# Low halves of the weight units of both attention stages: VectorE in one instruction of 1024 columns, in place of GpSimd in two of 512

## What is computed

```python
for i in range(DEPTH):
    h = rmsnorm(x, norm_g[i])
    mem_h = rmsnorm(mem, mem_norm_g[i])
    ...
    if i % 2 == 0:
        proj = jnp.einsum('bsd,de->bse', h, w_in_a[j])
        ...
        o_mix = mixer_dilated(qkv, qn_a[j], kn_a[j], ang_a)
    else:
        proj = jnp.einsum('bsd,de->bse', h, w_in_b[j])
        ...
        o_mix = mixer_axial_gqa(proj[..., :c1], proj[..., c1:c2], proj[..., c2:c3],
                                qn_b[j], kn_b[j], ang_b)
    ...
    o_mem = memory_attention(q_mem, mem_h, w_mem_kv[i], mem_qn_g[i], mem_kn_g[i])
    y = jnp.concatenate([o_mix, o_mem], axis=-1) * jax.nn.silu(gate)
    x = x + jnp.einsum('bse,ed->bsd', y, w_out[i])
```

## Time and profile before

| | |
|---|---|
| Median of 3 runs | 3570.39 us (3569.19 to 3571.53) |
| The profiled execution | 3569.75 us |
| Its span | 3567.8 us |
| TensorE busy | 3408.9 us (96%) |
| VectorE busy | 1560.0 us (44%) |
| ScalarE busy | 1321.2 us (37%) |
| GpSimd busy | 1412.1 us (40%) |
| Mean granted TensorE clock | 0.983 of full speed |

### The profile page before, as it was taken

The page is one execution under the profiler, slowest core; times in us unless marked ns, Lnnn a source line. Parts: engine busy times, 40 slices in busy tenths (PEclk is TensorE's granted clock), DMA queues, the critical chain, the costliest instruction groups (busy, mean ns, idle before and its releaser), DMA issues.

```text
span 3567.8 us, 45553 instructions
## 1 busy us (share of the span) xinstructions
PE 3408.9 (96%) x16418; PEld 2820.1 (79%) x16418; DVE 1560.0 (44%) x2613; ACT 1321.2 (37%) x2104; POOL 1412.1 (40%) x1040
## 2 busy tenths in 40 slices
PE   8999998899999999999889999989998999999898
PEld 7888876788888888887678888878787877877677
DVE  2221456542216422145654221653785387335633
ACT  3222435442225422243544222462442244444343
POOL 5554432145544454443314554343332432352122
PEclk9999999999999999999999999999999999999999
DMA  4223221023222222221102222222111211231111
GB/s 155 97 94 99 84 65 48 19 90 99 94 96 94 83 95 99 95 85 64 53 13 94 94 95 97 99 87 78 66 60 48 82 60 54 77 130 54 42 54 59
DMA packets 76659, 281.09 MB, mean 79 GB/s; under 512 B 8512, under 2 KB 8640, under 8 KB 76128
## 3 DMA queue, kind: packets, MB, share of 16 engines
q1 hardware_dynamic: 75600, 274.66, 23.2%
q10 hardware_dynamic: 912, 4.39, 0.4%
HBM read 276.92 MB, written 2.10 MB: 78 GB/s over the span
## 4 chain that ended last, share of the span: by engine, by line
PE 87%; DVE 8%; ACT 3%; issue 2%; DMA 0%; DVEq 0%; ACTq 0%; SPq 0%
PE ps L1765 16%; PE ps L1767 16%; PE ps L1766 16%; PE ps L1837 4%; PE ps L1838 3%; PE ps L1839 3%; PE ps L2301 3%; PE ps L2287 2%; PE ps L1876 2%; PE ps L1874 2%; PE ps L1875 2%; PE ps L2227 1%; PE ps L2348 1%; PE ps L2229 1%; PE ps L2228 1%
## 5 line engine op out<-in xcount | busy, mean ns | idle before, releaser
L536 POOL TENSOR_TENSOR w_lo<-raw,w_hi 128x512 fp32r<-128x512 f32 x1028 | 1400.5, 1385 | 2132.2 <-ACT w_hi L587 2132.1
L1765 PE MATMUL ps<-x_hi,w_hi 128*128 128x512 f32 x2560 | 1049.7, 410 | 4.6 <-issue 4.6
L1767 PE MATMUL ps<-x_hi,w_lo 128*128 128x512 f32 x2560 | 1000.1, 391 | 0.0
L1766 PE MATMUL ps<-x_lo,w_hi 128*128 128x512 f32 x2560 | 999.2, 390 | 0.0
L587 ACT ACTIVATE w_hi<-raw 128x1024 fp32r<-128x1024 f32 x514 | 542.2, 1057 | 1084.3 <-PE ps L1767 596.5
L1765 PEld LDWEIGHTS ps<-x_hi,w_hi 128*128 128x128 f32 x2560 | 483.2, 189 | 126.4 <-issue 29.5
L1766 PEld LDWEIGHTS ps<-x_lo,w_hi 128*128 128x128 f32 x2560 | 483.0, 189 | 118.5 <-issue 22.4
L1767 PEld LDWEIGHTS ps<-x_hi,w_lo 128*128 128x128 f32 x2560 | 481.5, 188 | 102.1
L1204 DVE TENSOR_TENSOR T<-T,ps 128x512 f32<-128x512 f32 x88 | 60.5, 687 | 660.1 <-PE ps L1767 650.8
L708 ACT ACTIVATE T<-ps 128x512 f32<-128x512 f32 x88 | 52.6, 598 | 359.5 <-PE ps L1767 354.6
L1874 PE MATMUL ps<-h_hi,w_hi 128*128 128x512 f32 (+1 forms) x440 | 153.2, 348 | 0.0
(11 more groups left out here) (327 smaller groups left out, 5205.9 us busy)
## 6 DMA issues: line engine op xcount, KB each, us to landing
raw<-in_weights SPq DMA_DIRECT2D x514, 512.0 KB, 3.3
Y<-in_x_t SPq DMA_DIRECT2D x1, 2048.0 KB, 7.9
mem<-in_mem_t ACTq DMA_DIRECT2D x2, 1024.0 KB, 7.1
out_t<-Y SPq DMA_DIRECT2D x8, 256.0 KB, 2.2
ple_p<-in_p_t ACTq DMA_DIRECT2D x2, 512.0 KB, 5.2
mat<-in_mats SPq DMA_DIRECT2D x1, 768.0 KB, 11.7
masks<-in_masks ACTq DMA_DIRECT2D x1, 576.0 KB, 8.0
rope<-in_rope_b ACTq DMA_DIRECT2D x1, 512.0 KB, 8.6
```

The costliest lines, as they stand in the source:

```text
L536: ins = pool.tensor_tensor(g.wl[:, k, part], g.raw[:, k, part], g.wh[:, k, part], ALU.subtract)
L1765: mm(out, wh[:, c], xh[:, kc, :], start=kc == 0, stop=False)
L1766: mm(out, wh[:, c], xl[:, kc, :], start=False, stop=False)
L1767: ins = mm(out, wl[:, c], xh[:, kc, :], start=False, stop=kc == DC - 1)
```

## The change

VectorE gets its own `low(u)`: it waits for the high half of the unit, subtracts all 1024 columns in one instruction and counts `lo_ready` up. `attend` calls it as `low(op.u + 4)` for each unit of the plan, behind the groups in the unit's middle and ahead of the copy of the unit's tile. GpSimd leaves these units out: in stage A the units from the tenth to the ninth from the end (90 units), in stage B the same (30 units). Before its first, VectorE waits until GpSimd has made the units ahead; GpSimd goes on when `lo_ready` has reached the end of the stretch. The ring, the plans, ScalarE, TensorE and SP are as before.

```diff
--- before.py
+++ after.py
@@ -321,6 +321,13 @@
 
 GATES_BEFORE, EARLY = 8, 5
 
+
+def vector_units(i):
+
+    u0 = BASE["AB"][i]
+    return u0 + 10, u0 + (U_A, U_B)[i] - 8
+
+
 PLANS = (between(plan_a()), between(plan_b()))
 
 
@@ -561,6 +568,11 @@
             q = g.CV[:, 0:4, n * P:(n + 1) * P]
             pool.tensor_tensor(q, q, g.EG[:, n, :].rearrange("p (h q) -> p h q", h=4), ALU.mult)\
                 .then_inc(s.qdec_done, 1)
+    for i in range(2):
+        first, last = vector_units(i)
+        low_many(at, first)
+        pool.wait_ge(s.lo_ready, last)
+        at = last
     low_many(at, N_UNITS)
 
 
@@ -1673,8 +1685,15 @@
             v.tensor_tensor(g.OL[:, t - 1, :], g.O[:, t - 1, :], g.OH[:, t - 1, :], ALU.subtract)\
                 .then_inc(s.olo_done, 1)
 
+    def low(u):
+        k = u % RING
+        dve.wait_ge(s.hi_ready, u + 1)
+        v.tensor_tensor(g.wl[:, k, :], g.raw[:, k, :], g.wh[:, k, :], ALU.subtract).then_inc(s.lo_ready, 1)
+
     def attend(i):
         dve.wait_ge(s.arena_landed, 16 * ARENA_LANDED[i])
+        dve.wait_ge(s.lo_ready, vector_units(i)[0])
+
         def item(op):
             if isinstance(op, Group):
                 group(op)
@@ -1688,6 +1707,7 @@
                 for mid in op.mid:
                     if isinstance(mid, Group):
                         item(mid)
+                low(op.u + 4)
                 if op.kind == "a_v" and op.t % 4 == 3:
                     dve.wait_ge(s.unit_done, op.u + 1)
                     if op.t == 15:
```

## The result

The changed kernel takes **3670.07 us** (median of 4 runs, 3668.62 to 3676.03) against 3570.6 for the kernel before on the same chip: a ratio of **1.0283, 95% interval 1.027 to 1.0295**, so 99.5 us slower. The forecast was 3647, 76 us slower: the sign and the range held, the sum came out 23 us short. The profiled execution of after is the 3676.03 (span 3674.0), 6 us over its median; what is counted in its trace adds up to 106.2, not 99.5.

What follows compares the result with a forecast made beforehand. TensorE was taken as the bound, with VectorE's queue the one that must not get later; seven terms of new TensorE idle time summed to 76.2 us on the profiled 3569.75, forecast 3647 us, range 3610 to 3700.

Steps and rivals of the forecast that it cites:

- step 3: Attention A's heads, 12 places with one unit between two groups: chain 1.1 us later, wait 0.76 each, 9.1 us.
- Step 4: A's first head, a group behind each of six units: a lap takes 8.9 us against 7.63, five laps, 6.4 us.
- Step 6: b_q units of B: 0.3 us later in one unit of a pair, about 0.8 in the other; four pairs, 4.4 us.
- step 1: Units with no group behind: sum of squares waits 1.2 us in 22 places, plus mem_k and A's last mem_q; 33.4 us.
- 2 V copies: Late copies of V hold banks the next unit writes: six places in A 13.4 us, one in b_v 1.6; 15.0.
- step 5: B's units with a group in the middle: 1.0 us three times, 0.4 for b_k, 2.3 before them; 5.7 us.
- 7 gates: Gates: group about 0.1 us late, B's twelve 1.2, plus 1.0 for the norm behind each stage's gate 0; 2.2 us.
- a rival at 0.12: Clock dips of 1.7 us at one in two of some 60 new TensorE waits: 76 + 50, 3697 us; chance 0.12.
- A under 0.97: Sign that the slower clock case holds: the granted clock of attention A falls under 0.97.
- faster rival: VectorE's relief from GpSimd wins: half of TensorE's waits for L1609 go and nothing comes, 3559 us; chance 0.06.

Runs made afterwards that it cites:

- unit_earlier: Changed kernel with VectorE's low half at the same place but for unit u + 3, whose high half was made a unit ago; 3543.98 us, ratio 0.9926.
- behind_norm: Changed kernel with the low half moved in VectorE's queue behind the tile's copy and the norm of the tile before; 3559.4 us, ratio 0.9968.

## Why the prediction was right in sign and short in size

**Right.** The bound was read rightly: VectorE's queue, not its load. The copy is 2.23 us late where the forecast said 2.3; the low half takes 1.225 us for the 1.21 forecast; the counts 788 and 120 are there; the rope products are at their least (L1586, the old L1574, at 0.679 us); L2368 waits in 30 places, 12 of them for 1.01 us and nine for 1.56 to 1.70; A's idle time is 84 us for "about 90", B's 43 for "about 45". The 76.2 us of the sum were meant as idle time of TensorE, and 72.6 us of new waits came. That they lie this close is in part luck: the list holds less of each wait than it costs (see below), and without the clock's 24 the profiled difference is 82 us, 6 over the sum, with step 3 and the places of no step too short and steps 4 and 6 too long. What the sum did not hold at all is the clock.

**By the steps.** Both traces are set side by side by the start of each unit's high half (L587, L599): how far after has fallen behind before, and by how much more at each unit. By this the steps cost:

| step | forecast | measured | what made the difference |
|---|---|---|---|
| 1 sums without group | 33.4 | 40.9 | 22 places at 1.25 to 1.28 (27.8 for 26.4); mem_k 4.2 and 4.4 for 2.5 a stage; last mem_q 4.5 for 2.0 |
| 2 V copies | 15.0 | 24.6 | 2.3, 3.7, 3.9, 3.8, 3.8, 3.3, and b_v 3.8 |
| 3 pairs of groups | 9.1 | 15.8 | 1.3 each for 0.76: three units of a later head fall back 2.56, of which 1.25 is step 1's |
| 4 first head | 6.4 | 5.0 | three laps at 1.1, two at 0.8, for 1.28 |
| 5 B, mem | 5.7 | 8.0 | the first, 4.9 for 2.3 |
| 6 b_q | 4.4 | 2.4 | 0.6 a pair for 1.1 |
| 7 gates | 2.2 | 2.4 | |
| in no step | - | 7.1 | 1.1 ahead of A's first unit, 2.3 at one unit of the second head, the rest in small steps around the first heads |
| sum | 76.2 | 106.2 | profiled executions |

**The step that failed is the sum's silence on the clock.** The forecast put the clock into a rival at 0.12, as 50 us on top, and none of it into the sum; its ground was that A's waits are short and A stands at 0.99. Steps 1, 2 and 5 have places where the wait is not 1.0 us but 1.9 to 3.7, and behind these the matmuls run at the lower level. The V copies are shown above. The mem_k unit of A is another, in the windows of after:

```profile
2386.00:2390.00 4.00, 2.73 (x18) 2.53 (x17) 1.47 (x2) 1.06 (x1) 0.00 (x0) 0.84 0.41 131
2390.00:2394.00 4.00, 3.40 (x14) 3.22 (x15) 0.88 (x3) 1.30 (x3) 0.00 (x0) 0.58 0.43 133
```

Its sum waits 1.86 us, the estimate's 1.8. The first window's 0.84 is not new: at the same place the kernel before shows 0.83 (2384.85 to 2388.85). The second is, before has 1.00 there: 0.42 x 4 = 1.7 us of clock, which is what the place costs over the 2.5 of the estimate. B's first group waits 3.73 us for the norm (1.44 before, 2.29 more, as step 5 has it), with 0.63 in 3301 to 3305 and 0.52 in 3305 to 3309. A's last mem_q is the third: its sum waits 3.73 us, with 0.53 in 2428 to 2432 and 0.62 in 2432 to 2436. The unit of the second head that no step holds is one more: its sum waits 2.91 us and the window from 2613 to 2617 stands at 0.63. Over their forecasts, these places are 9.6 us (V), 3.6 (mem_k), 2.5 (mem_q), 2.6 (B's first) and 2.3 (this one): 21 us, against the 24 that the clock's figures show. The rival named the mechanism and B's place; it was no alternative to the sum but a term of it. Its own mark, A under 0.97, was reached at 0.96, and half its 50 us came.

**Step 3** has a small slip in its own terms (1.1 less 0.4 is 0.7 a place, not 0.76), and it took its slack from a unit in which ScalarE's high half starts when the copy does. In many it starts later, behind ScalarE's rstd of the tile. From the timeline of after:

```profile
2697.63 0.63 ACT L626 ACTIVATE rstd<-rstd 128x512 f32<-128x512 f32 x1
2698.16 1.05 ACT L599 ACTIVATE w_hi<-raw 128x1024 fp32r<-128x1024 f32 x1
```

The high half has no idle time ahead of it: ScalarE was the one that was late. VectorE's low half follows at 2699.24 and the sum waits 1.58 us instead of 1.01. Step 4 had seen this order in the earlier trace rows; step 3 had not looked for it. **Step 6** had 0.3 for one unit of a pair, and that came four times at 0.32. The other, guessed at 0.8 without a row, was 0.14, 0.96, 0.71 and -0.66. **Step 4** had three of its laps 0.2 us and two 0.5 us too long; the cause was not looked for.

**The relief was undersized.** The forecast's faster rival had 11.7 us, half of the waits in the earlier trace rows, for GpSimd's silence; two pairs of runs say 31. The trace of unit_earlier shows the parts: 10.1 us off the waits for L1621 (23.3 to 13.2), and 15 us off the clock's account, (1 - 0.987) x 3541.2 = 46 us for 61. The same shortfall lies under the expectations of behind_norm and unit_earlier, which both came out faster than their ranges. The rival's direction was right for a kernel whose low half waits for something long done; the change isn't one, and the rival's condition ("if the high half were done before the copy is due") is exactly what unit_earlier makes true.

**The rule weighed.** In the earlier trace rows the rope product of two SBUF inputs takes 1655 ns at the median beside GpSimd's low halves; with GpSimd idle it takes 679. The Trainium skill (SBUF — State Buffer, section "Who interferes with whom") says that such a VectorE instruction and a GpSimd instruction that reads SBUF take turns; the trace agrees, with these numbers. The rule that the prediction weighed, of the Trainium skill (GPSIMD Engine Reference, section "Engine selection"), to put elementwise work on a tile on VectorE, gives a gain once the low half works on the unit before, 3544 us, and none where the change puts it.

**The last 10 us.** Some 10 us of the profiled 106.2 are in neither the list of waits nor the clock's figures, whose rounding is worth up to 3.6. The likely cause of most of it is that the list holds less of a wait than it costs. In the unit of 2890 above, the matmul ahead of the sum starts at 2892.28 and the sum at 2893.68, 1.40 us later where 0.23 is usual: 1.17 us lost, of which the list has 1.01, because the recorded end of a matmul lies behind the next one's start. The first matmul behind the sum then starts 0.56 us after it, 0.45 in before (2658.63 to 2659.08). Together this is 1.28, the shift of such a place in the table. The list has 78 waits and had 29; by an estimate from this one unit, 49 x 0.27 is 13 us, for the 10 to be explained.

**What stays open.** The first 1.1 us of the table's last row lie ahead of stage A and so are no work of the change. Why the profiled execution of after lies 5 to 7 us over its other three was not tried; that the lower clock comes behind a given wait in some executions only would be enough for it. When it comes is open even within one trace: behind two V copies of A the V unit waits 2.06 us each time (to 2460.2 and to 2489.6), the first place costs 2.3 us and the window behind it stands at 1.00, the second costs 3.7 with 0.62 in 2490 to 2494.

## What to carry to other kernels

Before work is moved onto an in-order queue, ask what it waits for and what is queued behind it, and only then how long it takes: the same 1.2 us a unit, 120 times, cost some 83 us behind a wait for a result just begun and 5 us behind one long done. If the ring of buffers allows, let the moved instruction work on the item before, or put it behind the copy that frees PSUM. And price each new wait of the matmul engine together with the clock behind it, wait by wait: here places with a wait of 1.0 us cost 1.3, and places with one of about 2 to 4 us often 1.5 to 1.7 us of clock on top.

## What was not expected of the hardware

- The granted clock fell right behind single waits of 1.9 to 3.7 us: to 0.58 in 2390 to 2394, 0.69 in 2809 to 2813, matmuls going from 0.39 to 0.63 us each. Three waits of 1.0 us a unit apart left it at 1.00 (2402 to 2422). It did not fall behind each longer wait: one of 2.06 us was followed by 0.62 and another of 2.06 us by 1.00. With matmuls run for nothing in the wait it stood at 1.00 in all four places, and they paid only where they were no longer than the wait.
- A wait without work exchanged one contention for another: with GpSimd's pair shifted against VectorE by 1.1 us, the norm went from 743 to 1264 ns and the rope product from 1655 to 680.
- VectorE's low half of 1024 columns took 1225 ns at the median, 0.01 us over the 1.21 us drawn from rows of 256 and 512 columns.
